# A two-layer encoder step on one core: the experts' slab splits, gather and scatter rearranged over PE, ACT, DVE and POOL, and the dense layer's weights made stationary

## The reference, cut to what matters

```python
def swiglu(h, wg, wu, wd):
    return (jax.nn.silu(h @ wg) * (h @ wu)) @ wd

def moe_swiglu(h, router, wg, wu, wd):
    probs = jax.nn.softmax((h @ router).astype(jnp.float32), axis=-1)
    top_p, top_i = lax.top_k(probs, TOP_K)
    ...
    for e in range(N_EXPERTS):
        out = out + combine[..., e:e + 1] * swiglu(h, wg[e], wu[e], wd[e])
    return out
```

## Time and profile before

| what | value |
|---|---|
| median of 3 runs | 1932.3 us (1927.3 to 1933.58) |
| the profiled execution's own time | 1932.11 us |
| its span | 1930.1 us |
| PE busy | 1692.9 us (88%) |
| DVE, ACT, POOL busy | 886.4, 670.4, 145.8 us |
| mean granted clock of PE | 0.945 |
| read from HBM | 329.43 MB |

### The profile page before, as it was taken

The page is one execution under the profiler, slowest core; times in us unless marked ns, Lnnn a source line. Parts: engine busy times, 40 slices in busy tenths (PEclk is TensorE's granted clock), DMA queues, the critical chain, the costliest instruction groups (busy, mean ns, idle before and its releaser), DMA issues.

```text
span 1930.1 us, 20990 instructions
## 1 busy us (share of the span) xinstructions
PE 1692.9 (88%) x7982; PEld 1269.0 (66%) x7982; DVE 886.4 (46%) x1194; ACT 670.4 (35%) x846; POOL 145.8 (8%) x243
## 2 busy tenths in 40 slices
PE   6997679768998999899867987879999999999996
PEld 5864457636787778687435764676766677666764
DVE  3672444243333232459135423364664456545653
ACT  4413123332322222242312232233554355434542
POOL 2340200000000000214011000000000000000000
PEclk9998799998999999899878999969999999999998
DMA  6643234172423332344432506248787888788883
GB/s 236 196 147 109 88 110 152 52 296 99 145 93 105 130 109 76 107 149 146 131 110 98 166 23 240 109 169 304 270 283 258 292 273 292 253 277 290 278 266 126
DMA packets 174557, 340.34 MB, mean 176 GB/s; under 512 B 6890, under 2 KB 48124, under 8 KB 174224
## 3 DMA queue, kind: packets, MB, share of 16 engines
q1 hardware_dynamic: 162224, 316.17, 48.4%
q0 software_dynamic: 3920, 12.58, 2.3%
q10 hardware_dynamic: 8352, 10.75, 1.7%
HBM read 329.43 MB, written 11.90 MB: 177 GB/s over the span
## 4 chain that ended last, share of the span: by engine, by line
PE 78%; DVE 10%; ACT 6%; issue 2%; DMA 2%; POOL 1%; ACTq 0%; DVEq 0%; POOLq 0%
PE bank L1030 16%; PE bank L1032 16%; PE bank L1031 16%; PE bank L1112 10%; PE bank L992 6%; PE bank L958 5%; PE bank L1131 3%; DVE arena_parts L722 2%; ACT arena_parts L718 2%; PE bank L1159 1%; ACT arena L1536 1%; PE bank L1441 1%; DVE arena L2271 1%; PE bank L1470 1%; DVE arena L2104 1%
## 5 line engine op out<-in xcount | busy, mean ns | idle before, releaser
L1030 PE MATMUL bank<-arena_parts,features_parts 128*128 128x512 f32 (+2 forms) x1344 | 527.2, 392 | 46.9 <-DVE arena_parts L722 22.4
L1032 PE MATMUL bank<-arena_parts 128*128 128x512 f32 (+2 forms) x996 | 391.4, 393 | 0.0
L1031 PE MATMUL bank<-arena_parts,features_parts 128*128 128x512 f32 (+1 forms) x960 | 369.3, 385 | 0.0
L1030 PEld LDWEIGHTS bank<-arena_parts,features_parts 128*128 128x128 f32 x1344 | 259.0, 193 | 102.1 <-issue 21.9
L722 DVE TENSOR_TENSOR arena_parts<-ring,arena_parts 128x2048 fp32r<-128x2048 f32 (+1 forms) x116 | 247.1, 2142 | 125.8 <-ACT arena_parts L718 125.8
L718 ACT ACTIVATE arena_parts<-ring 128x2048 fp32r<-128x2048 f32 (+1 forms) x116 | 206.7, 1796 | 113.7 <-PE bank L1032 112.9
L1032 PEld LDWEIGHTS bank<-arena_parts 128*128 128x128 f32 x996 | 193.2, 194 | 39.1
L1031 PEld LDWEIGHTS bank<-arena_parts,features_parts 128*128 128x128 f32 x960 | 184.4, 192 | 30.6
L1032 PE MATMUL bank<-arena_parts,features_parts 128*128 128x512 f32 (+1 forms) x480 | 180.4, 376 | 0.0
L1536 ACT ACTIVATE arena<-bank 128x512 f32<-128x512 f32 (+3 forms) x160 | 87.8, 563 | 253.4 <-PE bank L1032 140.3
L1031 PE MATMUL bank<-ring_low_parts,features_parts 128*128 128x512 f32 (+1 forms) x384 | 149.4, 389 | 0.0
(11 more groups left out here) (274 smaller groups left out, 1936.4 us busy)
## 6 DMA issues: line engine op xcount, KB each, us to landing
ring<-in_moe_w_up SPq DMA_DIRECT2D x40, 1024.0 KB, 5.2
ring<-in_moe_w_down SPq DMA_DIRECT2D x30, 1024.0 KB, 5.6
ring<-in_w_in SPq DMA_DIRECT2D x20, 1024.0 KB, 7.3
ring<-in_moe_w_gate SPq DMA_DIRECT2D x20, 1024.0 KB, 5.2
mem_kv<-in_moe_w_gate SPq DMA_DIRECT2D x20, 1024.0 KB, 5.3
ring<-in_cache_mem_k SPq DMA_DIRECT2D x16, 1024.0 KB, 6.3
ring<-in_cache_mem_v SPq DMA_DIRECT2D x16, 1024.0 KB, 6.0
ring<-in_moe_w_gate SPq DMA_DIRECT2D x20, 768.0 KB, 4.8
```

What stands on the lines that cost most here:

```text
L1030: nc.tensor.matmul(out, left[0], right[0], start=start, stop=False)
L1031: nc.tensor.matmul(out, left[0], right[1], start=False, stop=False)
L1032: return nc.tensor.matmul(out, left[1], right[0], start=False, stop=stop)
```

## The change

Five things change together; the rest of the program is as it was.

1. Dense layer: the weight block is the stationary operand and all 384 tokens are the moving one. A result has features on partitions, so it is the stationary operand of the down product as it stands: nothing is turned. ACT copies its high part (L1652 of the new file), DVE makes the low part.
2. Experts: the down product is a three-pass product too. All 18 slabs are split, and the turned activations as well. There are four part buffers in place of three.
3. Experts: h is written once to DRAM; the rows of a unit are fetched by an indirect DMA that POOL issues during the unit before, from row numbers that PE computes (`row_numbers`); a unit starts with 8 transposes in place of 48 gather products.
4. Experts: the scatter of a unit's result (with the splitting of the second half of its down product) is done inside the next unit. The first unit is written out ahead of the loop and has no scatter; one more scatter follows the last unit (`last_scatter`, `last_results`), with the final norm in between its tiles.
5. Experts: POOL does `split_low` of slabs 3, 7, 12 and 15 (`BY_POOL`), and the order of events is a list written by hand (`routed_events`) in place of the derived one.

```diff
+ROUTED_PARTS = 4
+BY_POOL = (3, 7, 12, 15)
...
+def routed_events():
...
+    return (split(0) + [("down", 1), ("gather", 0), ("gather", 1)] + split(1, 2) + scatter(0, 0) + split(3)
+            + scatter(0, 1) + [("gate", 0)] + split(4) + scatter(0, 2) + split(5) + [("up", 0), ("ST",)]
+            + scatter(1, 0) + split(6) + [("gate", 1)] + split(7) + scatter(1, 1) + scatter(1, 2) + split(8)
+            + [("up", 1)] + split(9) + [("aT", 0), ("S",)] + split(10) + [("gate", 2)] + split(11, 12)
+            + [("row",), ("up", 2), ("aT", 1)] + split(13) + [("aT", 2)] + split(14, 15) + [("down", 0)] + split(16, 17))
...
+            def split_low_by_pool(self, pool, i, s):
+                pool.wait_ge(self.high, i * self.n_split + s + 1)
+                nc.gpsimd.tensor_tensor(self.part(s, 1), self.raw(s), self.part(s, 0).bitcast(F32),
+                                        ALU.subtract).then_inc(self.split["g"], 1)
...
-            with eng.Fori(0, NE) as i:
+            step(0, True)
+            with eng.Fori(1, NE) as i:
                 step(i)
...
+                                for f in range(FF_GROUPS[c][1]):
+                                    if g == 0:
+                                        L.begin(pe, i, kind, c, f)
+                                    out = bank[FF_BANKS[kind][f]][:, 0:TOK]
+                                    for k in range(4):
+                                        ins = matmul3(out, [q[:, k, f * P:(f + 1) * P] for q in wt],
+                                                      [q[:, 4 * g + k, :] for q in hT_parts], g + k == 0, g + k == 4)
...
-                        if kind == "down":
-                            ins = nc.tensor.matmul(out, left[:, k, :], wt[:, k - k0, :], start=start, stop=stop)
-                        else:
-                            ins = matmul3(out, [q[:, k, :] for q in left], [q[:, k - k0, :] for q in wt], start, stop)
+                        ins = matmul3(out, [q[:, k, :] for q in left], [q[:, k - k0, :] for q in wt], start, stop)
...
+            def row_numbers(b):
+
+                for t in range(NT):
+                    ins = nc.tensor.matmul(b[:, 0:4], S_r[:, t, :].bitcast(F32), row_of[:, t:t + 1].to_broadcast([P, 4]),
+                                           start=(t == 0), stop=(t == NT - 1))
+                return ins
...
+            def take_rows():
+                pool.indirect_dma_start(rows_e, None, h_rows, bass.IndirectOffsetOnAxis(row_u[:, 0:1], 0)).then_inc(s_rows_in, 16)
+
+            def routed_step(i, first=False):
+                L = routed
+                for s in BY_POOL:
+                    if s == 15:
+                        L.wait_emptied(pool, i, "row")
+                        G.tensor_tensor(full[:, 15:16], minus_half[:, 0:1], minus_half[:, 1:2], ALU.add)
+                        take_rows()
+                    L.split_low_by_pool(pool, i, s)
+                pool.wait_ge(s_rows_in, i * 16 + 32)
```

More of the change, by code:

```diff
@@ L68 @@
                       ("smask", 4 * P), ("cmask", P),
-                      ("before", P), ("ones", P), ("slots", P)):
+                      ("before", P), ("ones", P), ("slots", P), ("row", NT)):
     CONST[_name] = (_at, _width)
@@ L253, in psum_jobs @@
             one(("pos", l), "v")
+            one(("row", l), "v")
         big[0] = 0
@@ L296, in slabs @@
     return out
+FF_BANKS = {"gate": (0, 1, 2, 3), "up": (4, 5, 6, 7), "down": ((3, 7, 0), (4, 5, 6))}
 def dense_jobs():
[L301 to L310, removed]
+    jobs = []
+    for c in range(3):
+        for kind in ("gate", "up"):
+            jobs.append(((kind, c, "first"), (), None))
+            jobs += [((kind, c, f), (FF_BANKS[kind][f],), "a" if kind == "gate" else "v") for f in range(FF_GROUPS[c][1])]
+    for c in range(2):
+        for g in range(3):
+            if g < 2:
+                jobs.append((("down", c, "part", g), (), None))
+            else:
+                jobs += [(("down", c, t), (FF_BANKS["down"][c][t],), "v") for t in range(NT)]
     return jobs
@@ L319, in dense_slabs @@
             for half in range(2):
-                out.append((kind, 4 * half, 4, c0, w, (kind, c, 0 if half == 0 else NT - 1)))
+                out.append((kind, 4 * half, 4, c0, w, (kind, c, FF_GROUPS[c][1] - 1 if half else "first")))
     for c in range(2):
         for g, (k0, nk) in enumerate(FF_GROUPS):
-            out.append(("down", k0, nk, 512 * c, 512, ("down", c, 0 if g < 2 else NT - 1)))
+            out.append(("down", k0, nk, 512 * c, 512, ("down", c, "part", g) if g < 2 else ("down", c, NT - 1)))
@@ L324, in dense_slabs @@
     return out
+ROUTED_PARTS = 4
+SCATTER_BANK = {(0, 0): 2, (0, 1): 1, (0, 2): 3, (1, 0): 4, (1, 1): 5, (1, 2): 6}
+BY_POOL = (3, 7, 12, 15)
 def routed_jobs():
-    jobs = [(("gather", 0), (6,), "v"), (("gather", 1), (7,), "v"), (("ST",), (6,), "a")]
+    jobs = [(("gather", 0), (6,), "v"), (("gather", 1), (7,), "v")]
+    jobs += [(("scatter", c, t), (SCATTER_BANK[c, t],), "v") for c in range(2) for t in range(NT)]
     for c in range(3):
         for kind in ("gate", "up"):
-            jobs += [((kind, c, "first"), (), None), ((kind, c), (2 * (kind == "up") + c % 2,), "a" if kind == "gate" else "v")]
-        if c:
-            jobs.append((("aT", c - 1), (T[c % 2],), "a"))
@@ L337, in routed_jobs @@
-    jobs += [(("down", 0, 0), (), None), (("down", 0, 1), (), None), (("aT", 2), (T[1],), "a"), (("down", 0), (4,), "v"),
+            jobs.append(((kind, c, "first"), (), None))
+            if (kind, c) == ("up", 2):
+                jobs.append((("row",), (7,), "v"))
+            jobs.append(((kind, c), (2 * (kind == "up") + c % 2,), "a" if kind == "gate" else "v"))
+        if c == 0:
+            jobs.append((("ST",), (7,), "a"))
+        else:
+            jobs.append((("aT", c - 1), ((7, 6)[c - 1],), "v"))
@@ L549, in hybrid_encoder @@
         minus_half = const("minus_half")
-        before, ones, slots = const("before"), const("ones"), const("slots")
+        before, ones, slots, row_of = const("before"), const("ones"), const("slots"), const("row")
         filled = sem("psum_filled")
@@ L2309, in _ @@
                     dense_steps(half_ffn)
-            for t in range(NT):
-                norm_row(3 * DEPTH, t)
         @block.gpsimd
@@ L2457, in _ @@
                 else:
+                    routed.prime(G.memset(full[:, 14:15], 0.0), "split_by_pool")
+                    for t in range(NT):
+                        pool.wait_ge(s_h, NT * (3 * l + 2) + t + 1)
+                        pool.dma_start(h_rows[t * P:(t + 1) * P, :], htok[:, t, :]).then_inc(s_hrows, 16)
                     gain(6)
+                    st.did(G.memset(rows_e, 0.0))
+                    st.settle()
+                    pool.wait_ge(s_hrows, 16 * NT)
+                    wait_emptied(pool, "row", l)
+                    take_rows()
+                    units(pool, routed_step)
                 rstd(3 * l + 3)
```

305 lines of the change are left out of this document (185 added, 120 removed).

## The result

The changed kernel takes 1960.28 us (median of 4 runs, 1957.97 to 1963.52), beside 1931.87 us for the kernel before on the same chip: a ratio of 1.0152, 95% interval 1.0129 to 1.0175. It is **slower by 1.5%**. The profiled execution took 1963.52 us, with a span of 1961.3, so 31.2 us more than the span before.

What follows compares the result with a forecast made beforehand. It took PE's own work to bound the units. From 1932.1 us it added 49.1 for the later last product, then subtracted 0.6 for the tail and 32.2 for the dense layer: 1948 us, range 1890 to 1972.

Steps and rivals of the forecast that it cites:

- PE's work in a unit, 51.6: Experts' units: PE's own work after the change comes to 51.6 us; if that were all, a unit would be 11 us shorter.
- The waits: Experts' units: PE waits 12.6 us a unit in ten places, the longest 4.4 to 4.5 us for slab 7.
- Restarts: Experts' units: restarting PE after a wait costs 0.1 us, 1.1 in all; with work and waits 65.3 us a unit.
- POOL's slab, 4.5: Experts' units: POOL's low part of a 2048-column slab takes 4.5 us, by a line through operations of 128 and 512 columns.
- The exclusion: Shared ports: POOL and DVE operations with two SBUF inputs keep each other out; 65.3 us a unit, 64.8 side by side.
- The clock: Experts' units: the clock falls once a unit, behind the wait for slab 7, costing 1.7 us: 67.0 a unit.
- rival 1: Slower still: clock falls twice as long, or again behind slab 15's wait; 1.7 more a unit, 1965 us; chance 0.17.
- Start of the units: First expert unit: rows arrive at 1291.5, and the unit begins in effect at 1292.0.
- The dense layer: Dense layer: fewer transposes, waits and clock falls, less some 0.9 us a half for restarts, save 32.2 us together.
- At nothing: Writing h to DRAM and the units' indirect row transfers cost no time; rows are needed some 25 us after issue.
- Rival 3: Faster: POOL does a slab in about 2.7 us, no clock fall follows, a unit takes 61.4: 1892 us; chance 0.20.
- Rival 4: Experts' units: PE does its 51.6 us without waits, about 1779 us; chance 0.02.

Runs made afterwards that it cites:

- e5: Changed kernel with all low parts on DVE and a new order of events, splits ahead of the results of the slab before: 1809.85 us.
- e1: Changed kernel with all 18 low parts of a unit on DVE, none on POOL, order of events kept: 1905.63 us.
- e4: Kernel before with only the dense layer of the changed kernel, its own experts' units kept: 1901.44 us.
- e9: As e6 (POOL's four slabs, new order), with DVE's six-column copy and the 0/1 matrix moved ahead of split 10: 1828.89 us.
- e8: As e7 (slab 12 alone on POOL), with DVE's six-column copy and 0/1 matrix ahead of split 10, turned chunk 0 ahead of split 11: 1821.72 us.
- e7: Nearly the order of e5 with slab 12 alone on POOL, six-column copy, 0/1 matrix and turned chunk 0 behind splits 10 and 11: 1869.93 us.
- e2: Changed kernel with gate of chunk 1 moved behind the split of slab 7; POOL keeps its four slabs: 1919.78 us.
- e6: Changed kernel with POOL's four slabs in a new order of events, six-column copy and 0/1 matrix behind split 11: 1882.34 us.

## Why the prediction was right

The forecast was 1948 us, slower, by the wait for slab 7 and the fall behind it. It came out slower by the same mechanism, at 1960, the upper end of what the prediction called the likeliest case alone (1938 to 1960).

- **PE's work in a unit, 51.6.** e5 shows it: a period of 53.10, 0.57 of it a wait, with 52.53 us of PE busy. Right within 1 us. The 11 us that it is under 62.6 compare it with a whole period, waits included; PE's busy time fell by 8 (60.47 to 52.53).
- **The waits.** Before slab 7 4.28 us (forecast 4.4 to 4.5), slab 12 1.9 (2.0), slab 14 0.95 (1.1), slab 15 2.36 (2.4), scatter 0.57 (0.8), one of 0.68 in place of 0.9 and 0.5 before slabs 10 and 11. The small one before slab 3 does not show. Each is right or a little high: PE's idle time in the second unit is 10.9 us, where the sum had 12.6 ("in ten places", of which its list has nine).
- **Restarts, too low, and luck in the 65.3.** PE's busy time in e1 without a fall is 53.87 us, 1.3 above e5's, with four more waits: an estimate of 0.3 us for a restart, where the sum had 0.1. In the changed kernel, 57.45 us busy less 3.1 for the two falls, work and restarts are some 1.6 us over the 52.7 of the sum, and the waits 1.7 under theirs. The two misses cancel, so that 65.3 and e1's 60.9 came out to 0.1 is in part luck.
- **POOL's slab, 4.5.** Undisturbed 4.51 to 4.59; the mean of 4.84 holds waits for DVE. The line through 128 and 512 columns in the earlier trace rows held out to 2048.
- **The exclusion.** DVE's low part of 1.76 us became 4.80 beside POOL. Right; its reach to the small copy was missed, and the changed kernel's order happens to keep that copy away from POOL's slabs (0.17 us there).
- **The clock: the term that was mis-sized.** The prediction expects "the fall once a unit: half of 3.4 us, 1.7", and from it 67.0 a unit. It falls twice, also behind the 2.36 us before slab 15. With 1.54 for one (e1: 60.96 and 62.50) that is 68.3 - 3.1 = 65.2 without falls, where the sum had 65.3. That is rival 1 in its second form. Its price for the second fall, 1.7, was nearly right, its time of 1965 was 5 too high, and it had a chance of 0.17.
- **Start of the units.** The transposes of the first unit start at 1257.7, where 1291.5 - 32.2 = 1259.3 was forecast. But the first unit has waits of 4.3, 1.9 and 2.2 with a fall behind each, of 6.8, 3.4 and 3.4 us, and ends 2.4 us later than the 1326.8 of the sum. With 9 x 1.3 that makes 14.1 us, all of the distance of the last product (1943.9) from the forecast (1962 - 32.2 = 1929.8).
- **The tail**: +0.2 for -0.6. **The dense layer**: -32.3 for -32.2, and alone -32.4 (e4). By the medians of e4 it is 27.4 us (23 to 31), so the last few us of it are not settled.
- **At nothing**: the row transfers in the units are never waited for, and none of e1 to e9 has such a wait but in the first unit (5.3 to 5.5 us), which the sum counts.
- **Rival 3** (faster, POOL in 2.7 us) fell with the 4.5. **Rival 4** (PE does its work without waits) is what the changed code can do in another order: e5. Its total had a slip: 1812 for the last product is 100.9 under 1912.9, so 1932.1 - 100.9 - 0.6 - 32.2 = 1798, not 1779; e5 took 1810.

## What to carry to other kernels

When one event in a hand-written queue waits for a product, everything behind it on that engine waits too. So compute for each slab when its high part can start, its low part ends and PE is there, and place the work that the next product needs ahead of the results of the last one: this was worth 96 us (e1 against e5), three times the dense layer's change. Work given to POOL relieves DVE by less than that work where both read two tensors from SBUF: DVE is busy for 48.0 us of a unit in e1 and for 42.5 in the changed kernel, though the four low parts are 9.2 us of it; the time in which it is held counts as busy. A slab on POOL keeps such DVE operations out for 4.5 us, where DVE would do it in 2.3, and even a copy of six columns is caught. What that costs hangs on what stands behind the operation that is held: 0.8 us a unit in e8 and 6 in e7, with one slab on POOL in both. A wait of PE is to be priced with the fall of the clock that may follow it, here some 1.5 us for one of 3.4.

## What the runs showed of the hardware that was not expected

- The same wait is or isn't followed by the lower clock from unit to unit: 12 of 20 waits of 2.02 us (e1), and all ten of 4.28 us in the changed kernel. There the nine of 2.36 us between 1388 and 1935 all were, and of the waits of 1.9 us only that of the first unit (1.87); in e2, which has waits of 1.90 and 2.34 us too, some of either were and some not. No wait of 0.92 us or less in a unit was (e5, e8, e9).
- Behind PE's waits of 3.25 and 3.78 us (e6, e7) the lower clock lasted 6.8 us in eleven of the 20 units and 3.4 in the other nine. Behind the waits of 4.28 in the changed kernel it lasted 3.4 in all nine units of the loop.
- A DVE copy of six columns between SBUF tensors is held for all of POOL's 4.5 us (0.16 to 4.54). DVE operations that read one input from PSUM are not: 0.16 us for L2162 in e8, and 0.69 beside POOL for 0.68 without it for the low part of a 512-column result in the changed kernel (L794).
